# Three transformer blocks on one core: the split activations begin 64 bytes past a multiple of 256, the seven products' extra places 128 past one

## What is computed

```python
# block 1, shortened
x   = layer_norm(ALPHA * x + 0.5 * swiglu(x, w_gate, w_up, w_down))
mix = hybrid_mixer(x, ...)      # x @ w_in; attention; state space scan;
                                # gate * (y @ w_branch) for each branch, summed; @ w_out
x   = layer_norm(ALPHA * x + mix)
x   = layer_norm(ALPHA * x + 0.5 * swiglu(x, ...))
# block 2: x @ w_in, stick breaking attention, spatial gating, gated linear attention, FFN with a convolution
# block 3: x @ w_in, sparse attention, pooling, delta rule, MLP with a squared relu
```

## Time and profile before

| | before |
|---|---|
| runs | 3425.03, 3421.72, 3424.30 us |
| median | 3424.3 us |
| span of the profiled execution | 3420.3 us, 4.0 us under the median |
| TensorE busy | 3348.4 us, 98% of the span, 18576 matmuls |
| VectorE busy | 2278.8 us, 67% |
| ScalarE busy | 1593.4 us, 47% |
| GpSimd busy | 339.6 us, 10% |
| HBM traffic | 386.5 MB, 113 GB/s |

### The profile page before, as it was taken

How to read it: one execution, slowest core, us unless ns; L and a number is a source line. 1 busy time by engine, 2 the same in 40 slices (tenths; PEclk the granted TensorE clock), 3 DMA queues, 4 the chain that set the end, 5 groups by cost and what they waited for, 6 DMA issues and landing times. The chain is left out here.

```text
span 3420.3 us, 48737 instructions
## 1 busy us (share of the span) xinstructions
PE 3348.4 (98%) x18576; PEld 2856.2 (84%) x18576; DVE 2278.8 (67%) x3709; ACT 1593.4 (47%) x2932; POOL 339.6 (10%) x375
## 2 busy tenths in 40 slices
PE   8999999999999999999999999999999999999999
PEld 7998888877788899887887888888787888889987
DVE  6887474778447787853565576667465567678865
ACT  3565254454433455555324363346355243355654
POOL 1000200022010100022010100000000104222200
PEclk9999999999999999999999999999999999999999
DMA  6346312220334435520454242245410330142464
GB/s 218 109 149 206 111 49 64 91 69 25 104 102 137 157 108 170 173 73 25 160 161 143 75 134 97 96 165 168 122 38 26 109 99 26 38 148 81 136 200 157
DMA packets 107988, 386.48 MB, mean 113 GB/s; under 512 B 12060, under 2 KB 14764, under 8 KB 107504
## 3 DMA queue, kind: packets, MB, share of 16 engines
q1 hardware_dynamic: 101088, 364.86, 32.6%
q0 software_dynamic: 4528, 16.43, 1.5%
q10 hardware_dynamic: 2144, 2.10, 0.2%
HBM read 379.13 MB, written 4.21 MB: 112 GB/s over the span
## 5 line engine op out<-in xcount | busy, mean ns | idle before, releaser
L445 DVE TENSOR_TENSOR w_low<-ring,w_high 128x1024 fp32r<-128x1024 f32 (+1 forms) x481 | 591.3, 1231 | 496.3 <-ACT w_high L433 490.6
L433 ACT ACTIVATE w_high<-ring 128x1024 fp32r<-128x1024 f32 (+1 forms) x481 | 485.0, 1010 | 491.8 <-PE bank L469 212.8
L469 PE MATMUL bank<-x_low,w_high 128*128 128x512 f32 (+1 forms) x1712 | 654.9, 388 | 19.5 <-DVE w_low L445 13.0
L469 PE MATMUL bank<-x_high,w_low 128*128 128x512 f32 (+1 forms) x1712 | 641.4, 380 | 0.0
L469 PE MATMUL bank<-x_high,w_high 128*128 128x512 f32 (+1 forms) x1712 | 417.8, 381 | 0.0
L469 PEld LDWEIGHTS bank<-x_low,w_high 128*128 128x128 f32 x1712 | 323.1, 189 | 82.4 <-issue 17.6
L469 PEld LDWEIGHTS bank<-x_high,w_low 128*128 128x128 f32 x1712 | 323.4, 189 | 56.9 <-issue 3.6
L469 PEld LDWEIGHTS bank<-x_high,w_high 128*128 128x128 f32 x1712 | 304.6, 189 | 59.1 <-issue 4.8
L738 PE MATMUL bank<-w_low,x_high 128*128 128x512 f32 (+1 forms) x384 | 145.6, 379 | 3.6 <-ACT z_z L2102 1.5
L740 PE MATMUL bank<-w_high,x_high 128*128 128x512 f32 (+1 forms) x384 | 143.5, 374 | 0.0
L739 PE MATMUL bank<-w_high,x_low 128*128 128x512 f32 (+1 forms) x384 | 143.5, 374 | 0.0
(11 more groups left out here) (821 smaller groups left out, 8215.0 us busy)
## 6 DMA issues: line engine op xcount, KB each, us to landing
ring<-in_W SPq DMA_DIRECT2D x686, 512.0 KB, 3.5
X<-in_x POOLq DMA_DIRECT2D x1, 2048.0 KB, 9.7
x_spill<-X POOLq DMA_DIRECT2D x1, 2048.0 KB, 8.2
X<-x_spill POOLq DMA_DIRECT2D x4, 512.0 KB, 3.5
ring<-in_W SPq DMA_DIRECT2D x4, 432.0 KB, 4.0
out<-X SPq DMA_DIRECT2D x3, 512.0 KB, 5.5
const<-in_consts POOLq DMA_DIRECT2D x1, 1133.0 KB, 10.6
f_hid<-in_xT ACTq DMA_DIRECT2D x4, 256.0 KB, 8.2
```

What stands on the lines that cost most here:

```text
L433: ac.activation(b.UH[u.place][:, 0:u.K * u.n], u.src(), ACT.Copy).then_inc(*b.split.act.up("high", i))
L445: dv.tensor_tensor(b.UL[u.place][:, 0:n], u.src(), b.UH[u.place][:, 0:n].bitcast(F32), SUB).then_inc(*b.split.dve.up("low", i))
L469: i = pe.matmul(out, w[:, k, c], v, start=n == 0 and q == 0, stop=last and q == 3 * K - 1)
```

## The change

It moves the starts of buffers and nothing else: no instruction, wait or transfer is added, removed or put elsewhere. The core of the diff:

```diff
-        self.colt = a.take("cols", self.ncol)
+        self.colt = a.take("cols", self.ncol, past=3 * LINE)
...
-        self.XH = a.take("x_high", 8, 512, dtype=F32R)
-        self.XL = a.take("x_low", 8, 512, dtype=F32R)
+        self.XH = a.take("x_high", 8, 512, dtype=F32R, past=3 * LINE)
+        self.XL = a.take("x_low", 8, 512, dtype=F32R, past=3 * LINE)
...
-        self.place = [area.take(f"{tag}_unit", SLOT, dtype=F32R, past=LINE) for _ in range(2)]
+        self.place = [area.take(f"{tag}_unit", SLOT, dtype=F32R) for _ in range(2)]
...
-        self.YH = a.take("a1_yh", 8, 512, dtype=F32R)
-        self.YL = a.take("a1_yl", 8, 512, dtype=F32R)
+        self.YH = a.take("a1_yh", 8, 512, dtype=F32R, past=3 * LINE)
+        self.YL = a.take("a1_yl", 8, 512, dtype=F32R, past=3 * LINE)
...
-        self.XS = a.take("m1_xs", 4, 2048)
+        self.XS = a.take("m1_xs", 4, 2048, past=3 * LINE)
...
-        self.YXH = Area(b, xs_at).take("z1_yh", 4, 2048, dtype=F32R)
+        self.YXH = Area(b, xs_at).take("z1_yh", 4, 2048, dtype=F32R, past=3 * LINE)
...
-        self.YXL = a.take("z1_yl", 4, 2048, dtype=F32R)
+        self.YXL = a.take("z1_yl", 4, 2048, dtype=F32R, past=3 * LINE)
```

More of the change, by code:

```diff
@@ L2335, in __init__ @@
         self.nge, self.nones, self.neg, self.eye = (a.take(f"a2_{n}", 128, dtype=F32R) for n in ("nge", "nones", "neg", "eye"))
-        self.YAH, self.YAL = a.take("a2_yh", 4, 512, dtype=F32R), a.take("a2_yl", 4, 512, dtype=F32R)
+        self.YAH, self.YAL = a.take("a2_yh", 4, 512, dtype=F32R, past=3 * LINE), a.take("a2_yl", 4, 512, dtype=F32R, past=3 * LINE)
         rows4 = down_rows(4)
@@ L2343, in __init__ @@
         self.V = a.take("g2_v", 4, 512)
-        self.YBH, self.YBL = a.take("g2_yh", 4, 512, dtype=F32R), a.take("g2_yl", 4, 512, dtype=F32R)
+        self.YBH, self.YBL = a.take("g2_yh", 4, 512, dtype=F32R, past=3 * LINE), a.take("g2_yl", 4, 512, dtype=F32R, past=3 * LINE)
         self.WS = a.take("g2_w", 8, 128)
@@ L2368, in __init__ @@
         self.sq = [a.take("l2_sq", 128) for _ in range(2)]
-        self.YCH, self.YCL = a.take("l2_yh", 4, 512, dtype=F32R), a.take("l2_yl", 4, 512, dtype=F32R)
+        self.YCH, self.YCL = a.take("l2_yh", 4, 512, dtype=F32R, past=3 * LINE), a.take("l2_yl", 4, 512, dtype=F32R, past=3 * LINE)
         self.bcr = Branch(self.gb, "bc2", "w_in_2", 6160, "p_c_2", rows4, halves(self.YCH, self.YCL), self.merged,
@@ L3190, in __init__ @@
         self.pairs = [[(64 * j, 64), (64 * (j + 4), 64)] for j in range(4)]
-        self.YAH, self.YAL = a.take("a3_yh", 4, 512, dtype=F32R), a.take("a3_yl", 4, 512, dtype=F32R)
+        self.YAH, self.YAL = a.take("a3_yh", 4, 512, dtype=F32R, past=3 * LINE), a.take("a3_yl", 4, 512, dtype=F32R, past=3 * LINE)
         self.bn = Branch(self.gb, "bn3", "w_in_3", 3872, "w_branch_nsa_3", self.pairs, halves(self.YAH, self.YAL), self.merged,
@@ L3208, in __init__ @@
         self.pc = [a.take("p3_c", 528) for _ in range(2)]
-        self.YBH, self.YBL = a.take("p3_yh", 4, 512, dtype=F32R), a.take("p3_yl", 4, 512, dtype=F32R)
+        self.YBH, self.YBL = a.take("p3_yh", 4, 512, dtype=F32R, past=3 * LINE), a.take("p3_yl", 4, 512, dtype=F32R, past=3 * LINE)
         self.bp = Branch(self.gb, "bp3", "w_in_3", 4896, "w_branch_pool_3", rows4, halves(self.YBH, self.YBL), self.merged,
@@ L3235, in __init__ @@
         self.SZ = a.take("d3_z", 4, 512)
-        self.YCH, self.YCL = a.take("d3_yh", 4, 512, dtype=F32R), a.take("d3_yl", 4, 512, dtype=F32R)
+        self.YCH, self.YCL = a.take("d3_yh", 4, 512, dtype=F32R, past=3 * LINE), a.take("d3_yl", 4, 512, dtype=F32R, past=3 * LINE)
         self.sqz = [a.take("d3_sqz", 128) for _ in range(2)]
```

## The result

| | before | after | difference |
|---|---|---|---|
| runs on the same chip | 3421.72 to 3425.03 us (4) | 3453.26 to 3457.41 us (4) | |
| median | 3423.8 us | 3453.6 us | ratio 1.0085, 95% interval 1.007 to 1.0099 |
| span of the profiled execution | 3420.3 us | 3452.3 us | +32.0 |
| TensorE busy | 3348.4 us | 3378.8 us | +30.4 |

A forecast was written before the change was run, and what follows sets the result against it. It took TensorE's matmuls, one after the other, to bound the kernel; 8.5 + 7 + 1.5 = 17 us saved took the median from 3424.3 to 3407 us (chance 52%), with an 8-in-10 range of 3398 to 3437.

The forecast's parts named there:

- Step 4: 512-column matmuls, moving operand from 128 to 64, 5496 of them: no change taken; bounds +22 us and -37 us.
- Rival B: Common products and tensor_rows: 512-column streams do not settle with starts 64 and 128; 4 ns each, 3433 us; chance 22%.
- Step 1: Seven products: all 84 matmuls of a pair at 113.3 ns, 9.52 us instead of 9.71; 45 pairs save 8.5 us.
- Step 2: First tiles behind a norm, 1248 matmuls of 256 columns: 6.7 ns less each, 8.3 us, of which 7 taken.
- Step 3: Extra places as moving operands, from 192 to 128: 300 matmuls from 231 to 227 ns, 1.5 us saved with settling.
- Step 5: Tokens as stationary operand from 128 to 64, 960 matmuls of 512 columns and 192 of 288: 0, bounds -2 to +5 us.
- Rival A: 512-column matmuls: the start's price is paid once per matmul at any width, so 5496 gain 6.7 ns; 3371 us; chance 14%.
- Rival C: All matmuls: 113.3 against 120.0 ns comes from buffers or surroundings, not the start; nothing moves, 3424 us; chance 6%.
- Rival D: Seven products and first tiles: VectorE's weight split and token waits leave half the gain there; 3416 us; chance 6%.
- Step 6: cols, XS, YXH and YXL as targets of the other engines, and the added gaps: no change.

The follow-up runs named there:

- bare products: Separate kernel without the three blocks: 16 pairs of moving and stationary starts, 24-matmul tiles at 512, 256 and 384 columns; also called the bare grid; 631.1 us.
- versions by stages: Kernel before with tokens at 64 only around seven-product stages, extra places at 128: 3422.6 us, 0.9992; same plus four added matmuls at distance -64 per stage: 3422.5 us, 0.9988.

## Why the prediction was wrong

**What bounds the kernel** was read rightly. The span moved by what the matmuls cost, +32.0 us for TensorE's +30.4, and no engine came in between. It counted on one clock throughout, by the digits of the earlier trace rows, and the clock was not the same in both executions: about 6 of the 32.0 us. The 4.0 us that it puts around the span are also two things: the profiled execution of the kernel after took 3453.66 us for a span of 3452.3, so some 1.4 us lie around a span. With these the span of before makes 3421.7, the fastest of its kernel's four runs, and that is the rest.

**Step 4 failed: "I take no change" for 512 columns moving from 128 to 64.** Its price was 233.3 ns for 226.7, +6.7 ns, where no change was taken; 5496 x 6.67 ns would be 36.6 us, and 35.0 were measured (34 of the 230 tiles lie among other matmuls, were at 230.9 ns before and so rise by less). The other terms came to a few us beside it. Three things in the step were wrong.
- Its ground was that 256 columns at 64 and 512 at 128 cost the same per column, 0.443 ns, so that both had to be the same undisturbed stream. The equality says nothing of the kind. At the settled prices and 2.4 GHz, 256 columns cost 272 clocks at the distance -64 and 288 at 0, which is 16 and 32 over their columns; 512 cost 560 and 544, which is 48 and 32 over. At 384 it is 40 and 32. There is no price per column to carry from one width to the other.
- It held that a load at 128 beside a stream at 64 does "without harm" over 512 columns what it does over 256. The bare products show that the same distance helps one width and harms the other.
- Its upper bound, +4 ns, was the row at 192 over 128, the nearest unequal pair. That is the distance +64, here 228.9 to 231 ns; the change makes the distance -64, for which no row of 512 columns stood anywhere. The end of the range was 3437, and the result lies 17 us beyond it.

**Rival B was the right way out, and too small.** It named the place (every common product and every product with tokens stationary) and the side. It had 4 ns and 3433 us; 6.7 ns in the moving ones gives 3424 + 36.6 - 17 = 3443.6. Steps 1, 2, 3 and 5 fell short by 5.4, 6.8, 0.4 and 2.2 us (below), and the first row of the table stayed 1.6 below its 36.6; from the -17 + 36.6 that makes the +32.8 of the table, and the medians differ by 29.8. Its mechanism, a stream that does not settle, was not the right picture: at -64 the stream settles, to the digit and for hundreds of matmuls, on a dearer price. **Rival A** took the 13.3 ns above the columns as a fixed charge that -64 lowers at any width; the charge is there at the distance 0 (32 clocks at 256, 384 and 512), but -64 lowers it at 256 alone. **Rival C** is contradicted by the bare products: 16.33 and 16.80 us for the same 72 matmuls with one start moved. The Trainium skill, "TensorE: Matmul & The Clock Gate", section "Step-by-step: what each phase is for", has the moving operand and the weights come through two independent ports, so that a load takes nothing from the running matmul. What the prediction drew from it, that starts could not matter, fails by the same two numbers. **Rival D** did not occur: no waits on w_low came up in the seven products, and in the stretch of the earlier trace rows VectorE is busy 117.3 of 130 us.

```profile
100.00:230.00 130.00, 130.00 (x1148) 129.91 (x1148) 117.27 (x166) 78.58 (x141) 0.00 (x0) 1.00 0.34 113
```

The same 130 us hold 1148 matmuls where they held 1127, which is the 2% of step 1.

**Step 1** (-8.5 us) was right in its price, 113.3 ns and 9.52 us a pair, in two stages of three. The second stage stood at 117.7 ns and 9.89 us, 0.18 more than before. The three rows of the seven products give -3.2 - 1.8 + 1.9 = -3.1 us. The sums show what was missed. They had the distance -64 before the change too, and in the trace of before they ran at 113.3 ns in 43 of the 45 pairs, but at 117.8 in two: the first pair of the first stage and the first of the third. In both the matmul behind the first sum began only after 221 and 222 ns. The one of the first stage, 36 sum matmuls from the second product of sums to the tokens behind them:

```profile
86.64 0.28 PE L647 MATMUL bank<-f1s_sl,w_high 128*128 128x256 f32 x1
...
90.88 0.28 PE L647 MATMUL bank<-x_low,w_high 128*128 128x256 f32 x1
```

4.24 us, 117.8 ns each. So the second steady price stood in the trace of before; the prediction read one pair of the third stage, and it was at 113.3.

**Step 2** (-7 us) gave -0.2. Six of the seven openings began at 117.7, and five of these came to 113.3 only after a break in the stream, one not at all. The undisturbed matmuls (up to 125 ns) went from a mean of 119.8 to 115.4 ns, some 5.2 us for nearly 1200 of them, where the step had 8.3. The distances over 125 ns grew in number from 54 to 84 and gave about 5 us of it back. All of that growth is matmuls at the lower clock's price: 57 of them after and 25 before lie in stretches at 0.50 or in the start of the kernel at the same 213 ns, and what they cost above the upper level grew by some 4.0 us; the others, 27 against 29, in which something is waited for or another kind stands between, took 1.3 more. That is the 1.3 that the step had allowed for waits. In the second profile of the changed kernel, with 44 of that sort, the first tiles are 3.0 us below before instead of 0.2. **Step 3** (-1.5 us) was right, 226.7 ns and -1.1. **Step 5** (0, bounds -2 to +5) measured +2.2: 229 to 234 ns instead of 227. The distance is +64 there, as tokens at 64 lie under weights that move at 128. In the bare grid 228.9 is its settled price; the 233.3 of one product, in both profiles of the changed kernel, is a second one that the grid did not show, and the same product was at 228.9 in the version without the branch inputs. **Step 6** held.

**What stays open** is why the distance counts, what decides between the two steady prices (a wait or a few other matmuls can turn one into the other; the traces don't say which way), and whether a version better than both kernels can be had for certain. The two versions by stages came out at 0.9992 and 0.9988 of the time before, the second with an interval just under 1; a gain of 0.1% is less than what this document counts as a difference.

## What to carry to other kernels

A bound must come from the same width and the same distance between starts; a row of another width says nothing about the sign. Where a stream of matmuls is the bound, a bare grid of pairs of starts at each width in use is the thing to run before buffers are moved, and the counts of the kernel's matmuls decide what may be moved: here 5520 of 512 columns, with 6.7 ns to lose by a matmul, and 2868 of 256 columns that were not yet at that distance, with 4.6 to 6.7 ns to gain. Then look at more than one stage in the trace, and at the first pair of a stage, because one combination can hold a cheaper or a dearer rhythm for a whole stage. And compare the clock of two profiled executions by stretches, not by the page's digits, before a few microseconds are put down to the change.

## What the runs showed of the hardware

- Float32r matmuls in a stream, each with its own weights, cost 226.7 to about 235 ns at 512 columns, 173.3 to 176.7 at 384 and 113.3 to 120.0 at 256, at a granted clock of 1.00, by the distance between the starts of the moving and the stationary operand within 256 bytes. At 512 and 384 columns all sixteen pairs of four starts agree within each of the four distances, to 1 ns; at 256 they do but for -64.
- The best distance depends on the width: 0 at 512, -64 at 256 (+112 cost 113.3 ns too, in one stretch of 192 matmuls, and -112 in one of two).
- The same combination can run at one of two steady prices: 113.3 or 117.8 ns at 256 columns and -64, 226.7 or 233.3 at 512 and -16, 228.9 or 233.3 at 512 and +64. A price lasted for as long as a stage of 16 pairs and 1344 matmuls. Where it turned, a wait, transposes or matmuls at another distance lay between; four of them at the distance 0 turned it both ways in one execution.
- At a granted clock of 0.50 the same matmuls cost 426 to 427 ns at 512 columns and 213 at 256. Such stretches came in every profiled execution of the whole kernel, one to five of them, and were worth some 6 us between the two that are compared here.
